# Products with stationary tokens read their moving columns, and write PSUM, from the last column to the first

## Chip, cores and metric

One of the eight cores of a Trainium2 chip runs the whole program. The metric is the time of one execution on the device in microseconds (us), as the median of several runs.

## What is computed

The reference runs two transformer blocks in float32 over 256 tokens of width 2048. Cut to what matters here, it is a chain of projections of all tokens by large weight matrices, with small attention cores between them:

```python
def first_block(x, mem, ...):
    y = hybrid_mixer(x, w_in, ...)        # x @ w_in, two attentions, gates, @ w_o_dsa, @ w_o_moba, @ w_out
    x = layer_norm(ALPHA * x + y, ln_g[0], ln_b[0])
    y = mem_cross_attention(x, mem, ...)  # x @ w_q, mem @ w_kv, softmax, @ w_o
    x = layer_norm(ALPHA * x + y, ln_g[1], ln_b[1])
    y = swiglu(x, w_ffn_in, w_ffn_out)    # (silu(x @ w_g) * (x @ w_u)) @ w_ffn_out, inner width 5632
    return layer_norm(ALPHA * x + y, ln_g[2], ln_b[2])

def second_block(x, ...):                 # rmsnorm, x @ w_in, three attention branches of 4 heads,
    merged = jnp.sum(gates * up, axis=2)  # gates * (ys @ w_up), summed over the branches
    return x + merged @ w_out
```

## The kernel before

**Tiles.** P = 128 partitions, S = 256 tokens (R = 2 halves of 128), NB = 512 output columns per block. Every weight matrix is cut into groups: GK = 2 contraction tiles of 128 rows by 512 columns (`[128, 2, 512]`, 512 KB). SyncE loads a group into one of 4 slots of `stage`; ScalarE copies it to float32r as the high part (`w_hi`, line 1241), VectorE subtracts it from the original and keeps the remainder (`w_lo`, line 1705). The activations lie transposed, with the contraction on the partitions, and split in the same way (`x_hl`, or `oh`/`ol`, `om_h`/`om_l`, `ff_h`/`ff_l`, `y_h`/`y_l`). A product is then the sum of three: high by high, high by remainder, remainder by high.

**Two ways of multiplying.** Where the result is wanted with tokens on the partitions, the tokens are the stationary operand and the weights' columns move: `group` and `half_group` (line 643 on, matmul at line 656). For each half r of the tokens the accumulator is the PSUM bank `ps[:, ACC + r, :]`, and its 2 x 3 products of a group follow one another. Most of these are 512 columns wide; one block of 8 groups is 336 wide (`FIRST_W`). `by_halves` does several groups for the first half and then the same groups for the second. Where the result is wanted transposed, for the attention heads, `heads_block` keeps the weights stationary and lets the tokens move: 512 columns (both parts) at line 707, 256 (the high part) at line 710. These lines aren't touched.

**Order.** Each engine's program is written out by hand, and semaphores count groups: `hi` (ScalarE's split is done), `lo_done` (VectorE's is), `w_used` (the second half's last product has read the slot; ScalarE waits for it before it refills `w_hi`). The last product of a block signals the first half by `tile0_done`; the evictions answer by `tile_out0` and `tile_out1`, for which the first product of the next block waits. Hooks put the small products of the attentions (in other banks) between groups. The evictions and all other readers of `ps` and of the weights' slots read columns from the first to the last.

**One other turned pattern.** At line 2394 VectorE copies a bias table from SBUF to SBUF with its columns from last to first (`bias4[:, h, lo:hi][:, ::-1]`), and at line 2397 copies it back in plain order.

Of the kernel before, what the change touches and what calls it, by code (L numbers as in the profile page):

```python
# [154 lines left out]
def some(value):  # L155

    return not isinstance(value, int) or value > 0


def two_blocks(nc, a, out, per):  # L160

    ctx = ExitStack()
    with ctx:
# [5 lines left out]
        def sem(name):  # L169
            if name not in sems:  # L170
                sems[name] = ctx.enter_context(nc.semaphore("s_" + name))
            return sems[name]
# [102 lines left out]
        ps = ctx.enter_context(nc.psum_tensor("b_ps", [P, 8, NB], F32))  # L275
        ACC, TP, SC, AUX, PT, OT = 0, 2, 4, 5, 6, 7
# [359 lines left out]
        def _(pe):  # L636

            c = Counts("pe", per)
            mm, T = nc.tensor.matmul, nc.tensor.transpose

            def group(kt, first, last, hi, lo, n=NB):

                slot, _ = slot_of(c.base.get("g", 0) + c.local.get("g", 0))
                pe.wait_ge(sem("lo_done"), c.next("lo_done"))
                for r in range(R):
                    half_group(slot, r, kt, first, last, hi, lo, n)
                c.next("g")

            def half_group(slot, r, kt, first, last, hi, lo, n=NB):

                if first and some(c.value(f"tile_out{r}")):
                    pe.wait_ge(sem(f"tile_out{r}"), c.value(f"tile_out{r}"))
                for t in range(GK):
                    rows = slice(r * P, (r + 1) * P)
                    for k, (x, w) in enumerate(((hi, upper), (hi, rest), (lo, upper))):
                        ins = mm(ps[:, ACC + r, 0:n], x[:, kt + t, rows], w(slot)[:, t, 0:n],  # L656
                                 start=first and t == 0 and k == 0, stop=last and t == GK - 1 and k == 2)
                if r == 1:
                    ins.then_inc(sem("w_used"), 1)
                elif last:  # L660
                    ins.then_inc(sem("tile0_done"), 1)

            def by_halves(n, kt, first, last, hi, lo, ready=None):

                slots = [slot_of(c.value("g") + i)[0] for i in range(n)]
                for r in range(R):
                    for i in range(n):
                        if ready:
                            ready(r, i)
                        if r == 0:  # L670
                            pe.wait_ge(sem("lo_done"), c.next("lo_done"))
                        half_group(slots[i], r, kt + i * GK, first and i == 0, last and i == n - 1, hi, lo)
                c.next("g", n)
# [410 lines left out]
            for kt in range(2):  # L1084
                pe.wait_ge(sem(f"tile_out{kt}"), c.value(f"tile_out{kt}"))
                for h in range(H_MEM):
                    if kt == 0:
                        pe.wait_ge(sem("pt_ready"), c.next("pt_ready"))
                    ins = mm(mem_out[h], vmem[:, kt, h * HD:(h + 1) * HD],
                             mem_pt[h][:, kt * S:(kt + 1) * S], start=kt == 0, stop=kt == 1)  # L1090
# [1431 lines left out]
```

## Time and profile before

| | |
|---|---|
| median of 3 runs | 2231.52 us (2231.26 to 2232.51) |
| the profiled execution | 2231.99 us |
| its span in the trace | 2230.4 us |
| PE busy (matmul) | 2220.3 us, 10457 instructions |
| PEld busy (weight loads) | 1850.8 us |
| DVE / ACT / POOL busy | 1304.6 / 1053.9 / 178.5 us |
| HBM traffic over the span | 188 GB/s |

PE is TensorE's matmuls, PEld its loads of stationary operands, which overlap the matmuls. DVE is VectorE, ACT ScalarE, POOL GpSimd, SP SyncE. L656 is line 656. The end of a matmul in the trace is modelled and includes its way through the array, so neighbours overlap. In the page's slices each digit is a fortieth of the span, in tenths. The chain that ended last is followed back from the last instruction to whatever released each step.

### The profile page before, as it was taken

To read this page: it belongs to the slowest core of one execution; us is meant where nothing else is said; L and a number is where in the kernel's file an instruction comes from. 1 tells how busy PE (TensorE), PEld (TensorE's weight loads), DVE (VectorE), ACT (ScalarE), POOL (GpSimd) and SP (SyncE) were. 2 spreads that over 40 slices of the span, in tenths; PEclk is the share of its full clock that TensorE was granted. 3 is DMA by queue.
4 is the path that set the end of the run, shared out by engine and by line. 5 is a ranking of instruction groups with operands and counts; after the bars stand their busy time and mean duration, and the time that the engine had idled before them with its cause. 6 is when DMAs were issued, how large, how long until landed. Compare 5 with 4: busy or idle time off the path is not lost.

```text
span 2230.4 us, 29901 instructions
## 1 busy us (share of the span) xinstructions
PE 2220.3 (100%) x10457; PEld 1850.8 (83%) x10457; DVE 1304.6 (58%) x1589; ACT 1053.9 (47%) x1283; POOL 178.5 (8%) x187
## 2 busy tenths in 40 slices
PE   9999999999999999999999999999999999999999
PEld 8888888888888888888888888888888888888887
DVE  5556655666667754454545445566656655655674
ACT  4444445555444544443444334446445444545643
POOL 1000000001304220000000000003000000200020
PEclk9999999999999999999999999999999999999999
DMA  7755654656856466656665565654566656665554
GB/s 233 230 173 166 191 160 147 192 165 219 263 174 213 134 202 197 202 198 193 191 190 187 191 196 181 197 199 151 170 189 198 206 177 186 207 189 176 167 189 166
DMA packets 216873, 421.33 MB, mean 189 GB/s; under 512 B 15400, under 2 KB 19536, under 8 KB 215120
## 3 DMA queue, kind: packets, MB, share of 16 engines
q1 hardware_dynamic: 212928, 401.79, 57.0%
q0 software_dynamic: 3584, 17.83, 2.4%
q8 instruction: 57, 0.93, 0.2%
q10 hardware_dynamic: 272, 0.52, 0.1%
q14 instruction: 32, 0.26, 0.0%
HBM read 417.98 MB, written 2.11 MB: 188 GB/s over the span
## 4 chain that ended last, share of the span: by engine, by line
PE 98%; POOL 1%; DVE 1%; ACT 0%; DMA 0%; issue 0%; ACTq 0%; DVEq 0%; SPq 0%; POOLq 0%
PE b_ps L656 82%; PE b_ps L707 7%; PE b_ps L710 3%; PE b_ps L749 1%; PE b_ps L832 1%; PE b_ps L732 1%; PE b_ps L847 1%; POOL b_x_res L554 0%; PE b_ps L841 0%; POOL b_x_res L556 0%; PE b_ps L932 0%; PE b_ps L901 0%; PE b_ps L848 0%; DMA b_gate_a<-in_x 0%; DVE b_w_lo L1705 0%; PE b_ps L1133 0%
## 5 line engine op out<-in xcount | busy, mean ns | idle before, releaser
L656 PE MATMUL b_ps<-b_w_hi,b_x_hl 128*128 128x512 f32 (+1 forms) x4144 | 1312.7, 392 | 1.2 <-DVE b_x_hl L1780 1.1
L1705 DVE TENSOR_TENSOR b_w_lo<-b_stage,b_w_hi 128x1024 fp32r<-128x1024 f32 (+1 forms) x756 | 932.8, 1253 | 577.0 <-ACT b_w_hi L1241 573.8
L1241 ACT ACTIVATE b_w_hi<-b_stage 128x1024 fp32r<-128x1024 f32 (+1 forms) x758 | 790.3, 1054 | 677.3 <-PE b_ps L656 590.3
L656 PEld LDWEIGHTS b_ps<-b_w_hi,b_x_hl 128*128 128x128 f32 x4144 | 777.1, 188 | 159.2 <-DVE b_x_hl L1780 1.3
L656 PE MATMUL b_ps<-b_w_lo,b_x_hl 128*128 128x512 f32 (+1 forms) x2072 | 804.4, 388 | 0.0
L656 PEld LDWEIGHTS b_ps<-b_w_lo,b_x_hl 128*128 128x128 f32 x2072 | 389.5, 188 | 76.9
L707 PE MATMUL b_ps<-b_x_hl,b_w_hi 128*128 128x512 f32 x576 | 205.8, 402 | 0.2 <-DVE b_w_lo L1705 0.2
L710 PE MATMUL b_ps<-b_x_hl,b_w_lo 128*128 128x256 f32 x568 | 159.3, 281 | 0.0
L656 PE MATMUL b_ps<-b_w_hi,b_ff_h 128*128 128x512 f32 x344 | 134.1, 390 | 0.0
L656 PE MATMUL b_ps<-b_w_hi,b_ff_l 128*128 128x512 f32 x344 | 133.9, 389 | 0.0
L656 PE MATMUL b_ps<-b_w_lo,b_ff_h 128*128 128x512 f32 x344 | 133.9, 389 | 0.0
L707 PEld LDWEIGHTS b_ps<-b_x_hl,b_w_hi 128*128 128x128 f32 x576 | 108.7, 189 | 28.8 <-issue 3.2
L710 PEld LDWEIGHTS b_ps<-b_x_hl,b_w_lo 128*128 128x128 f32 x568 | 107.3, 189 | 0.0
L656 PEld LDWEIGHTS b_ps<-b_w_hi,b_ff_l 128*128 128x128 f32 x344 | 64.6, 188 | 13.5
L656 PEld LDWEIGHTS b_ps<-b_w_hi,b_ff_h 128*128 128x128 f32 x344 | 64.6, 188 | 13.4
L656 PEld LDWEIGHTS b_ps<-b_w_lo,b_ff_h 128*128 128x128 f32 x344 | 64.6, 188 | 13.2
L554 POOL TENSOR_TENSOR b_x_res<-b_x_res,b_vec_a 128x512 f32<-128x512 f32 x16 | 28.1, 1758 | 568.0 <-ACT b_x_res L1326 557.2
L1857 DVE SCALAR_TENSOR_TENSOR b_x_res<-b_x_res,b_ps 128x512 f32<-128x512 f32 (+1 forms) x48 | 33.0, 687 | 47.6 <-PE b_ps L656 47.1
L1373 ACT ACTIVATE b_logits<-b_logits,b_nmax 128x128 f32<-128x128 f32 (+1 forms) x48 | 21.5, 448 | 79.8 <-DVE b_nmax L1806 79.8
L656 PE MATMUL b_ps<-b_w_hi,b_oh 128*128 128x512 f32 x136 | 53.7, 395 | 0.0
L656 PE MATMUL b_ps<-b_w_hi,b_ol 128*128 128x512 f32 x136 | 53.0, 390 | 0.0
L656 PE MATMUL b_ps<-b_w_lo,b_oh 128*128 128x512 f32 x136 | 53.0, 389 | 0.0
(328 smaller groups left out, 1536.9 us busy)
## 6 DMA issues: line engine op xcount, KB each, us to landing
b_stage<-in_w_in SPq DMA_DIRECT2D x333, 512.0 KB, 4.1
b_stage<-in_w_ffn_in SPq DMA_DIRECT2D x176, 512.0 KB, 4.5
b_stage<-in_w_ffn_out SPq DMA_DIRECT2D x86, 512.0 KB, 4.0
b_stage<-in_w_out SPq DMA_DIRECT2D x64, 512.0 KB, 4.1
b_stage<-in_w_up SPq DMA_DIRECT2D x24, 512.0 KB, 4.0
b_stage<-in_w_o_dsa SPq DMA_DIRECT2D x16, 512.0 KB, 4.5
b_stage<-in_w_o_moba SPq DMA_DIRECT2D x16, 512.0 KB, 4.1
b_stage<-in_w_kv_mem SPq DMA_DIRECT2D x16, 512.0 KB, 3.6
```

The costliest lines, as they stand in the source:

```text
L554: pool.tensor_tensor(x, x, vec_a[:, cols], ALU.mult).then_inc(sem("pool_step"), 1)
L656: ins = mm(ps[:, ACC + r, 0:n], x[:, kt + t, rows], w(slot)[:, t, 0:n], start=first and t == 0 and k == 0, stop=last and t == GK - 1 and k ...
L707: mm(ps[:, bank, :], upper(slot)[:, t, cols], flat(hl[:, j * GK + t, :, :]), start=j == 0 and t == 0, stop=False)
L710: ins = mm(ps[:, bank, 0:S], rest(slot)[:, t, cols], hl[:, j * GK + t, 0, :], start=False, stop=last and t == GK - 1)
L732: ins = T(ps[:, TP + j // 2, (j % 2) * S + r * P:(j % 2) * S + (r + 1) * P], nat[:, r, j * P:(j + 1) * P], ident[:, :])
L749: ins = T(ps[:, TP + t % 2, kk * S + r * P:kk * S + (r + 1) * P], src[:, r, (2 * t + kk) * P:(2 * t + kk + 1) * P], ident[:, :])
L832: ins = mm(ps[:, SC, lo:hi], q[:, t * P:(t + 1) * P], keys(hi - lo), start=k == 0, stop=k == len(pairs) - 1)
L847: mm(ps[:, bank, col:col + S], v0, probs_t[:, 0:S], start=True, stop=False)
L1241: act.activation(upper(slot)[:, :, 0:n], landing(slot)[:, :, 0:n], ACT.Copy)\
L1373: ins = act.activation(logits[:, 0, lo:hi], logits[:, 0, lo:hi], ACT.Exp, bias=nmax[:, t:t + 1], accum_out=rsum[:, t:t + 1])
L1705: dve.tensor_tensor(rest(slot)[:, :, 0:n], landing(slot)[:, :, 0:n], upper(slot)[:, :, 0:n].bitcast(F32), ALU.subtract).then_inc(sem("lo_d ...
L1857: dve.scalar_tensor_tensor(out=x, in0=x, scalar=alpha, in1=ps[:, ACC + r, :], op0=ALU.mult, op1=ALU.add).then_inc(sem(f"tile_out{r}"), 1)
```

## The change

Both the output in PSUM and the moving operand of the matmul in `half_group` get the step -1 along their columns, so that column n of the weights is still written to column n of the accumulator, but the last column comes first. The stationary operand, the order of the products, the waits and the signals stay. The instructions of every engine stand in the same order as before.

```diff
@@ -653,7 +653,7 @@
                 for t in range(GK):
                     rows = slice(r * P, (r + 1) * P)
                     for k, (x, w) in enumerate(((hi, upper), (hi, rest), (lo, upper))):
-                        ins = mm(ps[:, ACC + r, 0:n], x[:, kt + t, rows], w(slot)[:, t, 0:n],
+                        ins = mm(ps[:, ACC + r, 0:n][:, ::-1], x[:, kt + t, rows], w(slot)[:, t, 0:n][:, ::-1],
                                  start=first and t == 0 and k == 0, stop=last and t == GK - 1 and k == 2)
                 if r == 1:
                     ins.then_inc(sem("w_used"), 1)
```

## Rows read from the trace of the kernel before

**Rows 1.** The page, busy us (share of the span) xinstructions of each engine

```profile
PE 2220.3 (100%) x10457; PEld 1850.8 (83%) x10457; DVE 1304.6 (58%) x1589; ACT 1053.9 (47%) x1283; POOL 178.5 (8%) x187
```

**Rows 2.** The page, busy tenths in 40 slices and the granted clock

```profile
PE   9999999999999999999999999999999999999999
...
PEclk9999999999999999999999999999999999999999
```

**Rows 3.** The page, chain that ended last, share of the span

```profile
PE 98%; POOL 1%; DVE 1%; ACT 0%; DMA 0%; issue 0%; ACTq 0%; DVEq 0%; SPq 0%; POOLq 0%
PE b_ps L656 82%; PE b_ps L707 7%; PE b_ps L710 3%; PE b_ps L749 1%; PE b_ps L832 1%; PE b_ps L732 1%; PE b_ps L847 1%; POOL b_x_res L554 0%; PE b_ps L841 0%; POOL b_x_res L556 0%; PE b_ps L932 0%; PE b_ps L901 0%; PE b_ps L848 0%; DMA b_gate_a<-in_x 0%; DVE b_w_lo L1705 0%; PE b_ps L1133 0%
```

**Rows 4.** Waits: waiter <- waited for: us in total, times, longest us

```profile
ACT b_w_hi L1241 <- PE b_ps L656: 590.3, 396, 3.4
DVE b_w_lo L1705 <- ACT b_w_hi L1241: 573.8, 437, 6.2
```

**Rows 5.** Groups of PE by form: xcount | busy us, mean ns | idle before

```profile
L656 PE MATMUL b_ps<-b_w_hi,b_x_hl 128*128 128x512 f32 x4080 | 1297.8, 394 | 1.2 <-DVE b_x_hl L1780 1.1
L656 PE MATMUL b_ps<-b_w_lo,b_x_hl 128*128 128x512 f32 x2040 | 794.3, 389 | 0.0
...
L656 PE MATMUL b_ps<-b_w_hi,b_x_hl 128*128 128x336 f32 x64 | 14.9, 315 | 0.0
```

**Rows 6.** Pieces of the chain, in order of time: start us, us, what

```profile
35.81 14.73 PE b_ps L656 x96
...
820.48 43.57 PE b_ps L656 x192
...
953.79 130.58 PE b_ps L656 x576
```

**Rows 7.** Windows of line 656: stretch, us, PE and PEld busy, clock, DMA, GB/s

```profile
953.79:1084.37 130.58, 130.58 (x576) 107.77 (x575) 1.00 0.60 194
820.48:864.05 43.57, 43.56 (x192) 35.70 (x191) 1.00 0.66 201
35.81:50.54 14.73, 14.73 (x96) 14.45 (x95) 1.00 0.81 240
```

**Rows 8.** Line 656, weight loads: duration ns min/median/max, first and last start

```profile
L656 PEld LDWEIGHTS b_ps<-b_w_hi,b_x_hl x4144: 186/188/193, 35.5 to 2226.6; 128*128 128x128 f32 x198
```

**Rows 9.** Timeline, the end: start us, us, instruction [idle before <-releaser]

```profile
2226.80 0.39 PE L656 MATMUL b_ps<-b_w_hi,b_x_hl 128*128 128x512 f32 x1
2227.23 0.69 DVE L1857 SCALAR_TENSOR_TENSOR b_x_res<-b_x_res,b_ps 128x512 f32<-128x512 f32 x1 [0.67 <-PE b_ps L656]
```

**Rows 10.** Groups of VectorE by form, the turned copies and the plain one

```profile
L2397 DVE COPY b_bias<-b_logits 128x384 f32<-128x384 f32 x4 | 1.4, 360 | 0.1
...
L2394 DVE COPY b_logits<-b_bias 128x256 f32<-128x256 f32 x4 | 1.1, 285 | 0.0
L2394 DVE COPY b_logits<-b_bias 128x128 f32<-128x128 f32 x4 | 0.9, 222 | 0.0
```

**Rows 11.** Timeline of PE, first, second and twelfth pair of lines 710 and 707

```profile
71.81 0.28 PE L710 MATMUL b_ps<-b_x_hl,b_w_lo 128*128 128x256 f32 x1
71.93 0.40 PE L707 MATMUL b_ps<-b_x_hl,b_w_hi 128*128 128x512 f32 x1
72.16 0.28 PE L710 MATMUL b_ps<-b_x_hl,b_w_lo 128*128 128x256 f32 x1
...
75.70 0.28 PE L710 MATMUL b_ps<-b_x_hl,b_w_lo 128*128 128x256 f32 x1
```

**Rows 12.** Groups of VectorE and ScalarE: the two splits of a weight group

```profile
L1705 DVE TENSOR_TENSOR b_w_lo<-b_stage,b_w_hi 128x1024 fp32r<-128x1024 f32 (+1 forms) x756 | 932.8, 1253 | 577.0 <-ACT b_w_hi L1241 573.8
...
L1241 ACT ACTIVATE b_w_hi<-b_stage 128x1024 fp32r<-128x1024 f32 (+1 forms) x758 | 790.3, 1054 | 677.3 <-PE b_ps L656 590.3 <-PE b_ps L710 52.5 <-DMA b_stage<-in_w_out 16.5
```

## The prediction

> **What bounds the kernel.** I read the page of the profile from the top down and then the trace where the change bites. The busy times say that TensorE's matmuls cover the whole span (2220.3 of 2230.4 us) while VectorE has 58% and ScalarE 47% [rows 1]. The slices show that share in each of the forty, at the full granted clock [rows 2]. So there is no stage in which another engine or the memory sets the pace. The chain that ended last says the same by line: 98% of it is PE, and line 656, the only line that the diff touches, holds 82% [rows 3]. The waits give the direction of the pressure: ScalarE waited 590.3 us for products of line 656 to free a weight slot, and VectorE 573.8 us for ScalarE [rows 4]. The suppliers wait for TensorE, not TensorE for them; its own idle time ahead of this line is 1.2 us [rows 5].
>
> **Price of one product now.** A matmul's own duration in the trace (394 and 389 ns, [rows 5]) includes the way through the array and overlaps its neighbours, so it isn't what a product costs. The chain's unbroken pieces are: 576 products in 130.58 us, 226.7 ns from start to start; 192 in 43.57 us, 226.9 ns; 96 products of 336 columns in 14.73 us, 153.4 ns [rows 6]. The same stretches stand at granted clock 1.00 [rows 7], which is 2.4 GHz. From 336 to 512 columns, 176 more, the interval grows by 226.7 - 153.4 = 73.3 ns, 0.416 ns a column: one column per cycle of 2.4 GHz. 512 columns are 213.3 ns of this; 13.4 ns are left over, and for 336 columns (140.0 ns) the same 13.4. So a product is **13.4 ns fixed and 0.4167 ns a column**, and the second part is exactly what the change touches.
>
> The line runs 682 groups of 12 (2 contraction tiles, 2 halves of the tokens, 3 products), 8184 in all, 96 of them 336 wide. Sum: 8088 x 226.7 = 1833.5 us and 96 x 153.4 = 14.7 us, together 1848.2 us or 82.9% of the span, which meets the chain's 82%. One nanosecond more on each product is 8.2 us of the end.
>
> **The change part by part.** (a) It removes nothing and adds no instruction, wait or transfer. Both patterns are turned, so column n still lands on column n; the reference's values and every reader stay. The 12 products of a group stand in the same order against the same semaphores: nothing is moved, 0 us. (b) The stationary operand is not turned. Its load takes 188 ns [rows 8] under a product of 226.7 ns, so 38.7 ns of slack lie over it, and its cost is 0. (c) The hand-over between two products of one accumulator: forwards, column 511 is written last and the next product starts at column 0; backwards, column 0 is last and 511 first. A given column is touched again after the same 512 columns, so the distance from one update of an element to the next stays. The semaphore comes with the last product of a half and its readers start only then, so for them neither order is earlier. 0 us. (d) The tail: the last product, one eviction of 0.69 us and the store [rows 9] wait for the end of the product, whichever column that is. 0 us.
>
> (e) What is left is the rate of a column when the address falls. The trace of before has no turned pattern on TensorE, so I bound it. The lower end is that the address's direction is invisible to the memories: 0 ns. The upper end is that each of the two sides delivers only one column in two cycles: 213.3 ns more for 512 columns, 140.0 for 336, so 8088 x 213.3 + 96 x 140.0 = 1738.6 us. The nearest row is VectorE's. Line 2394 copies 128 and 256 float32 columns from a source with step -1 in 222 and 285 ns; line 2397 copies 384 with step +1 in 360 ns [rows 10]. The turned copies grow by 63 ns for 128 elements, 0.49 ns each; carried on to 384 they give 348 ns, where the forward copy took 360. So this engine reads SBUF backwards as fast as forwards, at about two elements per nanosecond, where TensorE asks for 2.4. A halved rate would have shown: 0.98 ns an element puts the 256 wide copy near 347 ns, and it took 285. I take the row's answer, **0 us**, and keep the upper end for the rival. Not excluded by it: the row reads SBUF alone and writes forwards; PSUM written backwards appears nowhere in before.
>
> A rule of the Trainium skill bears on the read side ("Advanced Engine Details and Errata", SBUF Cachelines): accesses that follow one another within the same 16-byte line run at full speed. A falling walk through float32 visits the same four neighbours of a line one after the other, so by it the cost is 0 too; only the copies on VectorE show that here.
>
> **Sum.** All terms are 0. The profiled execution took 2231.99 us around its span of 2230.4, and the median of the three runs is 2231.52, 0.47 lower. The forecast stands on the median: **2231.5 us**. Its own range is 2227 to 2236, 0.2% to each side, which is about what a measurement of this kernel can tell from no change (0.2% is 4.5 us, or 0.55 ns on each product).
>
> **Rivals.**
>
> *Slower by the rate (the other side).* The place is the path from the array to the bank, or from SBUF to the array: if it takes two neighbouring columns at once only when the address rises, every column becomes an access of its own. In a kernel bound by TensorE there is no cover: price 1738.6 us, so 2231.5 + 1738.6 = 3970. It decides from the first product on, since any loss above 0.55 ns a product shows. For it: the column rate is already the highest that the clock allows, so a path that has to pair columns has no spare cycle. Against it: the turned copies [rows 10], though for the read only. A milder form (three cycles for two columns) would be half of it, 869 us, so about 3101. The Trainium skill has a rule that speaks for this one ("Advanced Engine Details and Errata", PSUM Cachelines): every two consecutive elements should be contiguous, and a non-contiguous pattern slows matmuls significantly. Whether step -1 counts as contiguous is not said; two neighbours still share an 8-byte line. Chance 0.16.
>
> *Slower by a fixed amount for each product.* The 13.4 ns are not a constant of the machine: the streams of lines 707 and 710 (512 then 256 columns, the weights stationary) run eleven pairs in 75.70 - 71.81 = 3.89 us, 353.6 ns a pair, where 320.0 for the columns and twice 13.4 would give 346.8 [rows 11]. Something costs 6.8 ns a pair there, 3.4 a product. If the turned start cost that, it is 8184 x 3.4 = 28 us, so 2259; if it cost a second fixed share of 13.4 ns, 110 us, so 2341. Chance 0.14, most of it at the low end.
>
> *Faster.* If some of the 13.4 ns were a conflict between the end of one product and the start of the next that the other order avoids, at most 110 us come back, so 2122; 3.4 ns would give 2204. The suppliers would follow: a group of 12 would last 2.56 us against 1.25 for VectorE's split and 1.05 for ScalarE's [rows 12]. Nothing in the rows says that direction matters to it. Chance 0.04.
>
> *The change does nothing.* If the turn were lost on the way to the chip, the time would be the same and no row could tell; it is in the first case's 0.66.
>
> **Numbers.** No change 0.66; slower 0.30 (0.16 + 0.14); faster 0.04. The range takes in the first case and the fixed cost up to 2341, together 0.80, and leaves out the rate and the gain: 2227 to 2341.
>
> **What would show it.** Right: 576 products in 130.6 us in an unbroken piece of the chain, 153.4 ns for 336 columns, loads at 188 ns, clock 1.00, and ScalarE's waits for line 656 near 590 us. Wrong by rate: an interval that differs more for 512 columns than for 336, in the ratio 512:336, and lines 707 and 710 as before. Wrong by a fixed cost: the same addition at both widths. If the loads themselves grew beyond 226 ns, it would be neither, but a conflict on the read side.

## The result, and the profile after

The changed kernel takes **2279.58 us** (median of 4 runs, 2279.02 to 2279.71), the kernel before beside it 2231.71: a ratio of 1.0214, 95% interval 1.0201 to 1.0226. It is slower by 2.1%, some 48 us. The forecast was no change, 2231.5; 2279.6 lies inside the range of 2227 to 2341, but the likeliest case was the wrong one. The profiled execution took 2279.64 us around a span of 2278.0, 47.6 us more than the span before.

The page of the changed kernel: busy time by engine, the slices of PE with the granted clock, and the chain that ended last.

```profile
PE 2268.2 (100%) x10457; PEld 1852.8 (81%) x10457; DVE 1306.2 (57%) x1589; ACT 1053.9 (46%) x1283; POOL 175.7 (8%) x187
...
PE   9999999999999999999999999999999999999999
...
PEclk9999999999999999999999999999999999999999
...
PE 97%; DVE 1%; POOL 1%; ACT 0%; DMA 0%; issue 0%; ACTq 0%; POOLq 0%; DVEq 0%
```

Against [rows 1 to 3] only PE has grown by more than 2 us, namely by 47.9; the instructions are as many, the clock is the same, and the engines behind it do what they did. The waits of the changed kernel (waiter, waited for, us in total, times, longest) say who passed the time on:

```profile
ACT b_w_hi L1241 <- PE b_ps L656: 627.0, 402, 3.5
DVE b_w_lo L1705 <- ACT b_w_hi L1241: 602.8, 439, 6.3
```

Both suppliers wait longer than in [rows 4], by 36.7 and 29.0 us. So the time comes from inside line 656. Its groups by form, and the loads of its stationary operand:

```profile
L656 PE MATMUL b_ps<-b_w_hi,b_x_hl 128*128 128x512 f32 x4080 | 1324.6, 401 | 1.1 <-DVE b_x_hl L1780 1.1
L656 PE MATMUL b_ps<-b_w_lo,b_x_hl 128*128 128x512 f32 x2040 | 810.8, 397 | 0.0
...
L656 PE MATMUL b_ps<-b_w_hi,b_x_hl 128*128 128x336 f32 x64 | 14.9, 317 | 0.0
```

```profile
L656 PEld LDWEIGHTS b_ps<-b_w_hi,b_x_hl x4144: 186/188/192, 35.3 to 2274.2; 128*128 128x128 f32 x198
```

The loads still take 188 ns [rows 8]. The price of a product shows in the unbroken pieces of the chain (start us, us, what):

```profile
35.59 14.72 PE b_ps L656 x96
...
831.30 44.81 PE b_ps L656 x192
...
968.34 134.41 PE b_ps L656 x576
```

576 products of 512 columns now take 134.41 us, 233.3 ns each, where they took 226.7 [rows 6]. The 96 products of 336 columns take 14.72 us, 153.3 ns, and took 153.4. That is the odd part of the result: neither a fixed cost of each product nor a cost of each column leaves the 336 wide ones untouched.

The sum closes. 8088 x 6.65 ns would be 53.8 us. But the plain kernel's products don't all sit at 226.7 ns: from the start of each 512 wide product of the line to that of the next product (7932 intervals before and 7933 after, those under 245 ns) the mean was 227.32 ns before and is 233.40 after, and 7932 x 6.08 ns = 48.2 us. All intervals that begin with a product of line 656 add up to 1873.0 us before and 1921.1 after, 48.1 us more; those of line 707 to 153.4 and 152.9.

### The profile page after: what moved, and what is told of

Read it like the earlier page. It is cut to its first block, busy times and chain, and to the rows that moved or that the text cites. A ratio compares the mean times of both kernels' runs of the same rounds, so it can differ in the third digit from the quotient of the medians.

```text
span 2278.0 us, 29901 instructions
## 1 busy us (share of the span) xinstructions
PE 2268.2 (100%) x10457; PEld 1852.8 (81%) x10457; DVE 1306.2 (57%) x1589; ACT 1053.9 (46%) x1283; POOL 175.7 (8%) x187
## 4 chain that ended last, share of the span: by engine, by line
PE 97%; DVE 1%; POOL 1%; ACT 0%; DMA 0%; issue 0%; ACTq 0%; POOLq 0%; DVEq 0%
PE b_ps L656 83%; PE b_ps L707 6%; PE b_ps L710 3%; PE b_ps L832 1%; PE b_ps L749 1%; PE b_ps L732 1%; PE b_ps L847 1%; DVE b_w_lo L1705 0%; POOL b_x_res L554 0%; PE b_ps L841 0%; PE b_ps L932 0%; PE b_ps L901 0%; POOL b_x_res L556 0%; PE b_ps L848 0%; DMA b_gate_a<-in_x 0%; DVE b_x_res L1874 0%
## 5 line engine op out<-in xcount | busy, mean ns | idle before, releaser
L656 PE MATMUL b_ps<-b_w_hi,b_x_hl 128*128 128x512 f32 (+1 forms) x4144 | 1339.5, 400 | 1.1 <-DVE b_x_hl L1780 1.1
L656 PE MATMUL b_ps<-b_w_lo,b_x_hl 128*128 128x512 f32 (+1 forms) x2072 | 821.0, 396 | 0.0
```

The source lines that it names most:

```text
L656: ins = mm(ps[:, ACC + r, 0:n][:, ::-1], x[:, kt + t, rows], w(slot)[:, t, 0:n][:, ::-1], start=first and t == 0 and k == 0, stop=last and ...
```

## The experiments

In the diffs `w(slot)[...]` (later `mov`) is the moving operand, `ps[...]` (later `out`) the output and `wt` the stationary operand.

**1 and 2. Which side: read or write?**

```diff
+                        ins = mm(ps[:, ACC + r, 0:n], x[:, kt + t, rows], w(slot)[:, t, 0:n][:, ::-1],
```

> Only the moving columns are turned; PSUM is written in plain order, so each product of line 656 leaves its columns in the wrong order (the output isn't the reference's). Theory R (the extra 6.65 ns of a 512 column product come from reading SBUF backwards): 233.3 ns from start to start in the unbroken pieces, about 2279 us. Theory W (they come from writing PSUM backwards): 226.7 ns and 2231 us. Theory B (each side costs something, or only the pair does): a value between, or both single kernels at 226.7 ns.

```diff
+                        ins = mm(ps[:, ACC + r, 0:n][:, ::-1], x[:, kt + t, rows], w(slot)[:, t, 0:n],
```

> Only the PSUM side is turned; the moving columns are read in plain order (columns of each product in the wrong order). Theory W: 233.3 ns and about 2279 us. Theory R: 226.7 ns and 2231 us. Theory B: a value between, or 226.7 ns here as in the kernel with only the read turned.

Measured: with only the read turned 2279.67 us, ratio 1.0216 (1.0199 to 1.0233); with only PSUM turned 2231.38 us, ratio 0.9999 (0.9990 to 1.0009). A piece of the chain of each, the read first:

```profile
34.81 14.72 PE b_ps L656 x96
...
967.57 134.41 PE b_ps L656 x576
```

```profile
35.20 14.72 PE b_ps L656 x96
...
953.04 130.58 PE b_ps L656 x576
```

Theory R stands, and W and B fall: the whole cost is in reading SBUF backwards. 134.41 and 130.58 us are to the digit the pieces of the changed kernel and of the kernel before. PSUM takes columns from the last to the first for nothing. The rule that the prediction held against the change, that a non-contiguous pattern slows matmuls significantly ("Advanced Engine Details and Errata" of the Trainium skill, PSUM Cachelines), is not borne out for step -1: the ratio is 0.9999.

**3 and 4. How does it depend on the width?** Both sides turned, and both plain, with the widths changing from group to group:

```diff
+                if n == NB:
+                    n = (512, 510, 508, 504, 500, 496, 488, 480)[kt // GK % 8]
```

> Both sides turned, and the products of the eight groups of a block are cut to 512, 510, 508, 504, 500, 496, 488 and 480 columns in this order (the columns beyond are left out of the sums). Read by group, from the intervals between starts. Theory F (the cost belongs to a product that covers its bank to the last column): 233.3 ns at 512 alone, and width/2.4 + 13.4 ns at the others. Theory Q (the interval is rounded up to a step, and turning adds a few cycles that cross a step at 512 but not at 336): a staircase, with the plain kernel's steps at other widths. Theory P (a cost that grows smoothly with the width beyond 336): a straight line from 233.3 down, steeper than 0.417 ns a column.

> The same widths with both sides in plain order, as the scale for the turned ones. Theories F and P: width/2.4 + 13.4 ns, 226.7 down to 213.4 at 480. Theory Q: a staircase too, its steps at other widths than in the turned kernel.

Measured, as means of the intervals between products of the same width: turned 233.6, 233.5, 231.6, 228.8, 227.3, 226.9, 222.4, 219.9 ns from 512 down to 480; plain 228.7, 226.9, 228.2, 226.8, 224.5, 223.4, 221.5, 216.8. (Whole kernels: 2240.14 and 2211.81 us, one run each.) Theory F falls, since 510 and 508 columns cost extra too, 6.6 and 3.4 ns. The difference goes up and down with the width (2.0 ns at 504, 3.5 at 496, 0.9 at 488, 3.1 at 480), which is against theory P. The plain kernel doesn't follow width/2.4 + 13.4 ns either: at 496 it would be 220.1, and 223.4 were measured. Theory Q fits in part. But the single intervals scatter over 10 ns within a group of 12, so this pair settles only that the width matters in no simple way.

**5 to 7. Mixed kernels.** The three put plain and turned reads side by side, the plain in the first half of the tokens, the turned in the second.

```diff
+                        if r == 1:
+                            mov = mov[:, ::-1]
```

> From here on only the read is turned, and in each group the first half of the tokens (r = 0) reads forwards and the second (r = 1) backwards, so one kernel holds both. Widths by group of a block: 512, 464, 448, 416, 384, 352, 320, 256 (the columns beyond are left out of the sums; those of r = 1 are in the wrong order). Theory Q (the interval is quantised and turning adds a few cycles): the surplus goes up and down with the width, with some widths at 0. Theory P (a cost that grows with the width beyond some width): 0 up to about 336, then rising towards 6.65 ns at 512. Theory C (the moving read and the load of the next stationary operand, 188 ns long, disturb each other when both are under way in the same direction): the surplus is there where the product is longer than the load, and vanishes from about 188 ns (416 columns) down.

For `orders` the kinds are, with `a` blocks:

```diff
+                        a = {2: 2, 3: NB // 4, 5: 8, 7: 32}.get(kind)
+                        if kind == 1:
+                            wt = x[:, kt + t, :].rearrange("p (n b) -> p n b", b=2)[:, :, r]
+                        if kind in (4, 6):
+                            m = P // 2 if kind == 4 else P // 4
+                            out, wt = out[0:m], wt[:, 0:m]
+                        if a:
+                            out = out.rearrange("p (a n) -> p a n", a=a)
+                            mov = mov.rearrange("p (a n) -> p a n", a=a)
+                            mov = mov[:, ::-1, :] if r == 0 else mov[:, :, ::-1]
+                        elif r == 1:
+                            mov = mov[:, ::-1]
```

> Width 512 throughout; eight kinds by group of a block, each in two forms (r = 0 and r = 1). Kind 0: forwards, backwards (226.7 and 233.3 ns expected by all). Kinds 2, 5, 7, 3: the moving columns in 2, 8, 32, 128 blocks (of 256, 64, 16, 4 columns); r = 0 takes the blocks from last to first, each forwards, r = 1 the blocks from first to last, each backwards. Theory L (the order inside a 16-byte line costs): r = 1 has 233.3 ns at every block size, r = 0 has 226.7. Theory M (the direction of the long walk costs): r = 0 has 233.3 for small blocks, r = 1 has 226.7. Theory S (only where the stream starts and ends counts): r = 0 with 2 blocks starts in the middle, r = 1 with 128 blocks starts at column 3, and both are near 226.7. Kinds 1, 4, 6 change the stationary operand: step 2, or only 64 or 32 columns of it (kind 4, 6; the rest of the outputs is left out), r = 0 forwards and r = 1 backwards. Theory C: the surplus of r = 1 over r = 0 changes with them and shrinks with fewer stationary columns. If only the moving stream counts: 6.65 ns in all three.

> Group 0 has 512 columns, groups 1 to 7 have 448 columns from column 1, 2, 3, 4, 8, 16, 64 on; r = 0 forwards, r = 1 backwards (the other columns are left out). Theory A (a stream that starts off the boundary of a line costs, as the backward one does at column 511): the forward reads from 1, 2, 3 are slower than from 4, 8, 16, 64 by some ns, and the backward ones change with the offset in the same way. If direction alone matters: all forward ones alike (200.1 ns by width/2.4 + 13.4) and all backward ones alike.

What they taught first was a flaw in their design. The plain half of kind 0, which is 226.7 ns in the kernel before, came out at 232.3 ns in the mix (the turned half at 233.9). A plain stream of 512 columns needs three to eleven products to settle. In the kernel before, the intervals after the attention products at 302 us run 235, 233, 236, 224, 231, 235, 229, 233, 230, 227, 227 ns; in the changed kernel, at the same place, 240, 231, 233, 234, 233, 233. Turned products settle within four. Six products a half are too few for the plain ones, so the plain figures of these three runs don't say where a plain stream settles, and their differences aren't used.

Two readings don't hang on that. The first is on theory C, from the weight loads of the turned half in `orders` (groups by form, kinds 4 and 6):

```profile
L674 PEld LDWEIGHTS b_ps<-b_w_hi,b_x_hl 128*64 128x64 f32 x256 | 34.5, 135 | 25.1
...
L674 PEld LDWEIGHTS b_ps<-b_w_hi,b_x_hl 128*32 128x32 f32 x256 | 27.8, 109 | 32.0
```

With 64 and 32 stationary columns the loads fell from 188 to 135 and 109 ns, and the turned products stayed at 232.9 and 233.2 ns: the turned value isn't tied to how long the next load is under way. With the stationary operand read at step 2 (kind 1) the turned half took 233.8 ns. The second is that 32 blocks of 16 columns, each turned, took 265.7 ns, far above either direction. The whole kernels took 1950.43, 2286.73 and 2090.18 us, one run each.

**8. Settled orders.** The kinds again, now one kind for a whole block of the program, so that 84 like products follow one another.

```diff
+                            a, d, m = kind
...
+                            if a == 1:
+                                mov = mov[:, ::d]
+                            else:
+                                out = out.rearrange("p (a n) -> p a n", a=a)
+                                mov = mov.rearrange("p (a n) -> p a n", a=a)
+                                mov = mov[:, ::-1, :] if d == 1 else mov[:, :, ::-1]
```

> 512 columns read in blocks of 256, 64, 32, 16, 8, 4 and 2 columns, one kind for a whole block of the program; either the blocks from last to first and each forwards, or the blocks from first to last and each backwards. Theory L (the order inside a 16-byte line): turned inside gives 233.3 ns at every size. Theory M (the direction of the walk over many lines): blocks from last to first with 4 columns or fewer behave as backwards, 233.3 ns; blocks of 4 or fewer turned inside behave as forwards, 226.7; large blocks (256) turned inside behave as backwards, large ones from last to first as forwards. Between them is a size at which both change over, and it says how much the read takes at a time.

Pieces of the chain; each kind has its line. L676 is plain and L678 turned. Blocks from last to first, each forwards: L680 (256 columns), L684 (64), L688 (16), L696 (4), L700 (2).

```profile
1459.79 13.64 PE b_ps L676 x60
804.03 19.61 PE b_ps L678 x84
827.24 19.09 PE b_ps L680 x84
962.28 19.06 PE b_ps L684 x84
1051.08 19.60 PE b_ps L688 x84
1236.10 19.61 PE b_ps L696 x84
600.59 19.61 PE b_ps L700 x84
```

Blocks from first to last, each backwards: L682 (256), L686 (64), L690 (16), L694 (8), L698 (4), L702 (2).

```profile
241.17 19.61 PE b_ps L682 x84
1006.40 19.61 PE b_ps L686 x84
1073.43 22.40 PE b_ps L690 x84
1121.79 19.58 PE b_ps L694 x84
1258.44 19.04 PE b_ps L698 x84
1346.06 19.04 PE b_ps L702 x84
```

84 products in 19.04 us are 226.7 ns, in 19.61 us 233.4. There are two values, and a changeover. Whoever turns 4 or 2 columns in place and walks forwards over them pays nothing (226.7); whoever turns 8 or more pays (233.1 to 233.4, and 266.7 at 16). From the other side, blocks of 64 and 256 columns taken from last to first, each forwards, are as fast as plain (226.9 and 227.3, products on the way to settling included); with 16 columns and fewer they are as slow as fully turned. Theory L falls and M holds: what costs is to walk downwards from one stretch of 16 bytes to the next, if it is done often enough. Blocks of 64 columns from last to first step down 7 times in a product and pay nothing, blocks of 16 step down 31 times and pay in full, so the price isn't proportional to the steps. The changeover doesn't lie at one size: 4 to 8 columns (16 to 32 bytes) on one side, and on the other, with the 32 column kind (232.4 ns) counted in, between 32 and 64. Theory S of the run `orders`, that only the place where a stream starts and ends counts, isn't fully excluded, since each kind has its own first and last column. It would have to tell a start at column 255 (L682, slow) from one at 256 (L680, fast), and it doesn't say why 16 turned in place cost 266.7.

**9. Settled widths.**

```diff
+                            width_, d = kind
+                            out, mov = out[:, 0:width_], mov[:, 0:width_][:, ::d]
```

> One width and one direction of the read for a whole block (all but its first group, which keeps 512 columns forwards), so a run of 80 or more like products shows the interval into which they settle. Widths 480, 448, 416, 384, 352, 336, 320, 256, each forwards and backwards in turn by block (the columns beyond are left out of the sums). Theory T (a product settles at its columns plus a whole number of steps of 6.67 ns; forwards two steps, 13.3 ns, backwards three, 20.0 ns, but two where the pattern fits): 6.6 to 6.7 ns between the directions at some widths, 0 at others, nothing in between, and 153.4 ns for 336 both ways. Theory P (a smooth cost): the difference falls steadily from 6.6 ns at 512 to 0 at 336.

Pieces of the chain, plain and turned in turn: 480 columns (L670, L672), 448 (L674, L676), 416 (L678, L680), 384 (L682, L684), 352 (L686, L688), 336 (L690, L692), 320 (L694, L696).

```profile
1251.12 13.01 PE b_ps L670 x60
735.19 18.48 PE b_ps L672 x84
798.01 17.02 PE b_ps L674 x84
239.21 17.35 PE b_ps L676 x84
1879.47 15.68 PE b_ps L678 x84
898.09 16.05 PE b_ps L680 x84
954.59 14.59 PE b_ps L682 x84
971.91 14.93 PE b_ps L684 x84
990.45 13.53 PE b_ps L686 x84
1006.72 13.63 PE b_ps L688 x84
1091.74 8.29 PE b_ps L690 x54
1107.51 12.88 PE b_ps L692 x84
557.25 12.32 PE b_ps L694 x84
1594.85 5.28 PE b_ps L696 x36
```

Per product that is, plain and turned: 216.8 and 220.0, 202.6 and 206.5, 186.7 and 191.1, 173.7 and 177.7, 161.1 and 162.3, then 153.5 and 153.3, 146.7 and 146.7. Two of the plain values depend on the block. Other blocks of the same kinds ran so, 416 columns (L678) and 352 (L686):

```profile
879.52 15.82 PE b_ps L678 x84
...
1024.23 13.45 PE b_ps L686 x84
```

These are 188.3 and 160.1 ns. At 256 columns, the last width of the edit, the chain runs through waits for weights for long stretches; the undisturbed series of 84 starts give 120.0 ns plain (after the first few) and 118.4 turned. The turned halves of `widths_two` agree: 191.1 ns at 416, 177.7 at 384, 147.1 at 320, 118.7 at 256.

So the cost of turning is 3.2 to 4.4 ns from 480 to 384 columns (2.8 at 416 against the slower plain block), 1.2 to 2.2 at 352, nothing at 336 and 320, and at 256 the turned read is 1.6 ns faster; with 6.7 at 512 it is largest where this kernel works. Theory T said all or nothing, 6.7 or 0: it falls as worded, since values between occur. But they are means of series that never lock to one interval and run through a pattern (211, 202, 211, 203 ns turned at 448; 176, 182, 175 turned at 384; 218, 215, 218, 216 plain at 480). Every plain or fully turned series that does lock, to within 1 ns, has either 13.3 or 20.0 ns left over its columns at 0.4167 ns each: 226.7, 173.3, 160.0, 153.3, 146.7 and 120.0 on one side, 233.3 and 220.0 on the other. Theory P (a steady slope) falls too, for the differences run 3.2, 3.9, 4.4, 4.0, 1.2, 0, 0, -1.6. And theory C, which had the surplus gone from 416 columns down, finds 4.4 ns there and 4.0 at 384.

**10. Settled offsets.** 448 columns from another first column on.

```diff
+                            o, d = kind
+                            out, mov = out[:, 0:448], mov[:, o:o + 448][:, ::d]
```

> 448 columns from column 0, 1, 2, 3, 4, 8, 12, 16, 32 and 64 on forwards, and from 0, 1, 2, 3, 4 and 16 on backwards, one kind for a whole block. Theory A (the start within a line or a larger unit decides): the forward read settles at 200.0 ns from 0, 16, 32, 64 and at 206.7 from some of 1, 2, 3, so a plain read can be as slow as a turned one; a backward read from a suitable column settles at 200.0. Theory D (direction alone): 200.0 for all forward ones and 206.7 for all backward ones.

Pieces of the chain, plain from columns 1 (L672), 3 (L676), 4 (L678), 8 (L680) and 16 (L684), then turned down to columns 1 (L692), 3 (L696) and 16 (L700).

```profile
769.94 13.43 PE b_ps L672 x65
239.47 16.81 PE b_ps L676 x84
908.21 16.80 PE b_ps L678 x84
927.78 17.36 PE b_ps L680 x84
1007.89 16.81 PE b_ps L684 x84
...
1170.12 17.36 PE b_ps L692 x84
1250.58 17.38 PE b_ps L696 x84
1291.69 17.35 PE b_ps L700 x84
```

All turned ones take 206.5 to 206.9 ns, wherever they begin. Among the plain ones shown, columns 3, 4 and 16 give 200.0 to 200.1, but columns 1 and 8 give 206.6 and 206.7, as slow as turned. Column 3 does so in each of its long blocks, and so do 1 and 8. 0, 12, 32 and 64 lie between (202.7, 203.2, 203.9, 202.7). Column 2 has no value of its own; two of its blocks (L674):

```profile
827.58 16.80 PE b_ps L674 x84
...
867.60 17.35 PE b_ps L674 x84
```

The first locks at 200.0 ns; the second, like three others of this kind, swings between 204 and 209 with a mean of 206.6. Column 4 has a second block too, at 202.4 ns instead of 200.0. So the same plain read can fall into more than one rhythm, and what decides between them is not shown.

Theory D falls: a plain read can have the same surplus. Theory A holds in half: the place where a plain read begins counts (3 against 1 and 8), but not by lines of 4 columns and not alone, and the turned read gets the fast value nowhere.

**11. Fours.** Both sides in groups of 4 columns, each backwards, the groups from first to last, so that each column still goes to its own place.

```diff
+                        fours = lambda t_: t_.rearrange("p (a n) -> p a n", n=4)[:, :, ::-1]
+                        ins = mm(fours(ps[:, ACC + r, 0:n]), x[:, kt + t, rows], fours(w(slot)[:, t, 0:n]),
```

> The whole of line 656 with both sides in fours: the 4-column groups from first to last, each read and written backwards. Theory M (only the direction of the walk from one 16-byte line to the next costs): 226.7 ns a product, 2231 to 2232 us, no change; if it settles sooner after the small products than the plain order does, as one block of the steady kernel hints, up to 5 us less. Theory L, or a cost of writing in broken runs of 4: at least 233.3 ns, 2279 us or more.

Measured: 2231.43 us (11 runs), ratio 0.9999 (0.9990 to 1.0008). No change, as theory M has it, with all 8184 products of line 656 in the new order. Writing PSUM in falling runs of 4 costs nothing either. The 5 us that one block had hinted at are not there.

**12. The other products turned.**

```diff
+                            mm(ps[:, bank, :][:, ::-1], upper(slot)[:, t, cols], flat(hl[:, j * GK + t, :, :])[:, ::-1],
...
+                                ins = mm(ps[:, bank, 0:S][:, ::-1], rest(slot)[:, t, cols], hl[:, j * GK + t, 0, :][:, ::-1],
```

> Line 656 as before; lines 707 and 710 (weights stationary, tokens move) turned on both sides instead. Before, a pair of them takes 353.6 ns, 6.8 more than two steps of 6.67 ns for each would give, so the plain reads there already take the slow value. Theory T (turning takes away the favourable case and adds nothing where a plain read doesn't have it): 353.6 ns a pair within 1 ns, 2231 to 2232 us. Theory D (each turned product of 512 columns costs 6.65 ns more than a plain one): 360 ns a pair, 640 x 6.65 = 4.3 us more, 2236 us.

Measured: 2232.48 us (11 runs), ratio 1.0003 (0.9994 to 1.0012). The timeline of PE, the first start of line 710 and the one eleven pairs later:

```profile
71.84 0.28 PE L710 MATMUL b_ps<-b_x_hl,b_w_lo 128*128 128x256 f32 x1
...
75.73 0.28 PE L710 MATMUL b_ps<-b_x_hl,b_w_lo 128*128 128x256 f32 x1
```

Eleven pairs in 3.89 us, 353.6 ns each, exactly as in [rows 11]. Over all 605 undisturbed pairs the mean went from 351.6 to 353.5 ns, 1.9 ns or 1.2 us in all. Theory D wanted 6.65 a pair. Where the plain read already stands near the slow value, turning it adds little. The pair before was not the constant that eleven pairs made it look: single pairs ranged from 345 to 360 ns.

## Why the prediction was wrong

*What bounds the kernel: right.* TensorE alone sets the pace; all of the 48 us came out at the end, and the suppliers waited longer by a like amount. The factor was right too: a nanosecond on each product was worth 8 us.

*The price of a product: right for this kernel, wrong as a law.* "13.4 ns fixed and 0.4167 ns a column" came from two widths, 512 and 336, and both happen to be among those where the plain stream settles at its best. At 384 columns it holds too (173.4 ns by the law, 173.3 once settled). But at 480 it gives 213.4 and 216.8 were measured, at 448 from column 0 it gives 200.1 and the stream took 202.6. Two points made a line on which not all the points between lie, and the view of the product as a rate and a constant hid the part that the change touches.

*(a), (b), (c), (d): right.* The loads kept their 188 ns, nothing moved, and the side of PSUM, with the hand-over between products, cost nothing (write only turned: 0.9999).

*(e): the step that failed.* The prediction took 0 ns from VectorE's turned copies. The row's answer, a read without loss backwards, carries over only to short products: 153.3 ns for 336 columns against 153.4, and 146.7 for 320 both ways. At 512 columns the time left over the columns was 13.4 ns and became 20.0. Whether the 6.65 ns are lost between two products or inside a long one is not shown. The copies come in twos and fours behind other work; they say nothing of a stream of products that overlap. The prediction wrote that PSUM written backwards appears nowhere in before, and looked for the risk there; it was on the side that it thought the row had answered.

*The rivals.* The halved rate (3970 us) didn't occur; its doubt about PSUM was unfounded. The fixed cost (2259 to 2341 us, chance 0.14) was nearest in size: 6.65 ns lies between its 3.4 and 13.4. Its evidence was the right one, that 13.4 ns is no constant since lines 707 and 710 lose 6.8 ns a pair more (4.8 over all 605 pairs); experiment 10 shows plain reads with that same surplus. But its own mark, the same addition at both widths, failed at 336. That the range held the result is therefore luck: it reached so far for a rival whose mechanism isn't the one measured. With hindsight the row said that this kernel has plain products that cost more, 5 to 7 ns a pair, so that the favourable 226.7 was a state that can be lost, and deserved more than 0.14.

*The Trainium skill's line rule* ("Advanced Engine Details and Errata", SBUF Cachelines), full speed for accesses that follow one another within a line of 16 bytes, gave 0 for the read. It holds inside a line: 4 columns turned in place are free (226.7 ns; 2231.43 us for the whole kernel). It doesn't speak of the direction from line to line, and that is where the cost was.

*What stays open.* Shown are the side (read), the scale (4 columns, 16 bytes, turned in place are free and 8 are not), that the write doesn't matter, and that the turned value doesn't change with the width of the stationary operand. Not shown is the mechanism: why the surplus vanishes at 336 columns and turns round at 256, why plain reads from columns 1 and 8 have it and those from 3 don't, why one from column 2 has it in some blocks only, why 16 column blocks turned in place jump to 266.7 ns.

## What to carry to other kernels

Let the moving operand's addresses rise; if a product's columns must be reversed, do it on the PSUM side, where it cost nothing here, or keep the read upwards over at least 64 columns at a time, or turn within 4. That is for products of 512 columns; those of 336 and fewer lost nothing. Before a change to the innermost pattern of a saturated TensorE is priced at nothing, look at the whole interval from product to product and not only at a copy's rate: with 8000 products each nanosecond there is 8 us. A price law for products should be checked at a third width.

## What the runs showed of the hardware that was not expected

- A stream of like plain products of 512 columns settles: after a break its intervals wander over 224 to 236 ns for three to eleven products and then lock at 226.7. Backwards it locks at 233.3 within four.
- 448 plain columns settle at 200.0 ns from column 3 and at 206.7 from column 1 or 8. From column 2 one block settled at 200.0 and four at a mean of 206.6.
- The surplus of the turned read depends on the width: 6.7 ns at 512 columns, 3.2 to 4.4 from 480 to 384, 0 at 336 and 320, and -1.6 at 256.
- Blocks of 16 columns, each backwards, walked upwards: 266.7 ns for 512 columns, 33 ns more than with blocks of 8 or 64.
